# First mixture of experts on gathered 64-row tiles: sixteen by expert, seven for overflow, two side by side

## Chip, cores, metric

One core of a Trainium2 chip runs a whole network forward for one sequence of 256 tokens of width 1024. The metric is the device time of one execution in microseconds (us). Lower is better.

## The reference, cut to what matters

The network is a first block (parallel attention mixer, cross attention to a memory, a hierarchical mixture of experts) and then two layers (a state-space layer and an attention layer), each followed by an expert-choice mixture. The change is in the mixture of the first block:

```python
p_group = jax.nn.softmax((h @ w_group).astype(jnp.float32), axis=-1)      # 4 groups
g_sel = jnp.argmax(p_group, axis=-1)
aff = jax.nn.sigmoid((h @ w_expert)...)                                    # 4 experts in each group
_, local = lax.top_k(aff_grp + bias_grp, TOPK_IN_GROUP)                    # 2 of them
...
for e in range(N_EXPERTS):                                                 # 16, width 256
    act = jax.nn.silu(h @ w_gate[e]) * (h @ w_up[e])
    y = y + combine[..., e:e + 1] * (act @ w_down[e]).astype(jnp.float32)
```

Each token has two experts with a weight above zero, so `combine` has 512 entries above zero out of 256 x 16. h is float32, and so are the weights: 1 MB each for gate, up and down of one expert.

## The kernel before, in words

The kernel is a row of blocks; at the end of each all engines meet. The mixture of the first block has two of them.

**The preparing block** (L1372 to L1515) normalizes X and transposes it into hT (NormT, L423 to L446), computes the router (L1409), works out the choice on VectorE in some 35 small dependent operations (L1462 to L1488), and beside that runs six pieces of an unrelated product, Ada (L763, L751, L783). Then hT is split into a high and a low fp32r part (L458, L461) and the weight of each token for each expert is spread over all partitions as cb by 32 small products (L1420) and eight copies.

**The expert block** (L1529 to L1667) takes every expert over all 256 tokens. Each float32 product is made of three fp32r products of high and low parts, high x low, high x high, low x high (matmul_split, L465 to L467). For one expert, gate_up (L1538) is 2 matrices x 2 halves of the width x 8 chunks of 128 rows x 3 = 96 products of 256 columns; down (L1551) is 2 token tiles x 2 column halves x 2 chunks x 3 = 24 products of 512 columns. PSUM banks Y collect all experts, beginning with X itself (L1535). VectorE splits every weight (L458, L461) and applies cb. SyncE loads the weights of later experts into three slots of 2 MB as old ones come free (L1646, L1652). The block runs as hardware loops over pairs of experts. At the end VectorE copies Y to X (L1635), and SyncE issues the first weights of the state-space block (load_weights, L323) before it reaches the end of the block.

**Helpers.** `Banks` (L101) hands out the eight PSUM banks in turn, and a bank may be filled again when the engine named at its opening has emptied it. `Ring` (L134) does the same for six weight slots of 2 MB: a piece is loaded when the piece before it in its slot has its `freed` mark. SyncE goes through the pieces in one fixed order, and a piece that isn't free yet holds up all behind it. NormT writes each token's normalized row to xn, and then the transposed rows with the gain to hT.

**The expert-choice mixture of the later layers** (L2376 to L2695) isn't changed, but its rows are used below: it already works on gathered tokens, in plain float32 products of 64 columns of stationary data by 512 moving columns, two of them side by side in the two column halves of the array (L2574, `tile_position=(0, 64 * n)`), with its gathering product at L2441 taking every fourth column of xn (`spread`) as stationary data.

Of the kernel before, what the change touches and what calls it, by code (L numbers as in the profile page):

```python
# [13 lines left out]
P = 128  # L14
# [24 lines left out]
CAP = 32  # L39

# [7 lines left out]
def constant_table():  # L48
# [13 lines left out]
    }  # L62
    f = np.float32(10000.0) ** (-np.arange(0, 32, 2, dtype=np.float32) / np.float32(32))
# [3 lines left out]
    parts["cos2d"], parts["sin2d"] = np.cos(ang), np.sin(ang)  # L67
    at, cols = 0, []
# [84 lines left out]
def build(nc, A, out):  # L153
# [15 lines left out]
    with ctx:  # L169
# [90 lines left out]
        gate_v = A["moe_w_gate"].rearrange("a e (k p) n -> p (a e) k n", p=P)  # L260
        up_v = A["moe_w_up"].rearrange("a e (k p) n -> p (a e) k n", p=P)
        down_v = A["moe_w_down"].rearrange("a e (k p) n -> p (a e) k n", p=P)

        weights(("moe1", 0), [(0, KD, D_EXP, gate_v[:, 0]), (2048, KD, D_EXP, up_v[:, 0])], among=3)
        weights(("moe1", 1), [(0, KD, D_EXP, gate_v[:, 1]), (2048, KD, D_EXP, up_v[:, 1])], among=3)
        weights(("moe1", 2), [(2048 * i, 2, D, down_v[:, i]) for i in range(2)], among=3)
        MOE1_SLOTS = [stream[-3 + j][2] for j in range(3)]
# [527 lines left out]
        with ExitStack() as scope:  # L795
# [100 lines left out]
            def _(act):  # L896
                act.dma_start(consts[:, :], A["consts"]).then_inc(ld["consts"], 16)
# [474 lines left out]
        with ExitStack() as scope:  # L1372
            xn = sb("xn3", [P, NT, D], scope=scope)
            wr = sb("wr", [P, KD, 20], scope=scope)
            lg = sb("lg", [P, NT, 20], scope=scope)
            R = {k: sb("r_" + k, [P, NT, 16], scope=scope) for k in ("aff", "score", "w", "one", "both", "m", "d")}
            comb = sb("comb", [P, NT, 16], scope=scope)
            combT = sb("combT", [16, S], scope=scope)
            cb = sb("cb", [P, N_EXP, S], scope=scope)
            gated = sb("gated", [P, 2, 512], scope=scope)  # L1380
            actT = sb("actT", [P, 2, 2, 512], F32R, scope)
            norm = NormT("n3", [X[:, t, :] for t in range(NT)], xn, hT, plain_gain("moe_norm_g"))
            to_combT = Transpose("combT", lambda n, t: comb[:, t, :], 1, 16, lambda g, m: combT[:, :].unsqueeze(1), by=(DVE,))
            wr_loaded, sub_ready, exp_ready, comb_ready = (sem(x) for x in ("wr_loaded", "sub_ready", "exp_ready", "comb_ready"))
            gu_full, silued, act_ready, down_done = (sem(x) for x in ("gu_full", "silued", "act_ready", "down_done"))
            gated_step = sem("gated_step")
            gu_split, down_split = sem("gu_split"), sem("down_split")
            gu_loaded = [sem(f"gu_loaded{j}") for j in range(2)]
            down_loaded = [sem(f"down_loaded{j}") for j in range(2)]
            h_high, h_low = hT_r[:, :, S:2 * S], hT_r[:, :, 0:S]  # L1390
            Y = [psum[i][:, :] for i in range(4)]
            GU = [[psum[4][:, :], psum[5][:, :]], [psum[6][:, :], psum[7][:, :]]]
            prep = scope.enter_context(ExitStack())
            ada_buf = sb("ada_buf3", [P, 2, 512], scope=prep)
            ada0, ada1 = Ada(ada_buf), Ada(ada_buf)
            block = prep.enter_context(nc.Block())

            @block.tensor
            def _(pe):
                ada0.tensor(pe)  # L1400
                norm.tensor(pe)
                pe.wait_ge(wr_loaded, 32)
                for t in range(NT):
                    b = banks.open(("router", t), DVE)
                    if b.emptied:
                        pe.wait_ge(*b.emptied)
# [8 lines left out]
                for e in range(0, N_EXP, 2):  # L1415
                    b = banks.open(("cb", e), (DVE, ACTE)[e // 2 % 2])
                    if b.emptied:
                        pe.wait_ge(*b.emptied)
# [10 lines left out]
            def _(act):  # L1429
# [7 lines left out]
                for e in range(0, N_EXP, 2):  # L1437
                    copy_out(act, ACTE, ("cb", e), cb[:, e:e + 2, :].rearrange("p e t -> p (e t)"), 512)
# [1457 lines left out]
```

## Time and profile before

| | us |
|---|---|
| median of 3 runs | 2513.43 (2509.4 to 2515.15) |
| the profiled execution | 2513.87 |
| its span, first to last instruction | 2512.1 |
| preparing block, from 397 | 42 |
| expert block, to the end of its last product | 281 (439 to 720) |
| last product to the first instruction of the next block | 8.1 |

All rows below are of the profiled execution. PE is the matrix engine's product, PEld its load of stationary data, which overlaps the product before it. DVE is VectorE, ACT ScalarE, SPq the queue of SyncE that issues transfers. A float32 product shows as two records of PE, an fp32r product as one. The duration of a record is longer than the distance between two starts, because the products are pipelined; where the text speaks of a pace, it is the distance. PEclk is the clock granted to the matrix engine as a share of 2.4 GHz: 1.00 is 2.4 GHz, 0.50 is 1.2 GHz.

### The profile page before, as it was taken

What the parts mean: (1) busy time and instruction counts of PE and PEld (TensorE: products, weight loads), DVE (VectorE), ACT (ScalarE), POOL (GpSimd) and SP (SyncE); (2) the same over time, 40 slices, a digit from 0 to 9 for tenths busy, and PEclk for the clock granted to TensorE, in tenths of its full rate; (3) what the DMA queues carried; (4) which work ended last, traced back from release to release, by engine and by line L of the source; (5) the groups of instructions that cost most, each with busy time, mean ns of one, the idle gap of its engine ahead of it and who ended that gap; (6) DMA issues with size and microseconds to landing.
All of it is one profiled execution on the core that took longest, in us unless ns stands there. A gap on an engine that the chain in (4) does not pass through costs nothing. (4 is left out here: it accounts for less than half of the span.)

```text
span 2512.1 us, 27445 instructions
## 1 busy us (share of the span) xinstructions
PE 2153.2 (86%) x10982; PEld 1279.0 (51%) x10982; DVE 1106.7 (44%) x1572; ACT 653.5 (26%) x1197; POOL 43.3 (2%) x55
## 2 busy tenths in 40 slices
PE   7965988999959899999879888888769879888886
PEld 5733444899958788888653222222334433222222
DVE  4576233777757889884431222222247321111112
ACT  4232122000025667674211111111105211111110
POOL 0000000000000000000000000000010000000000
PEclk9968997999988999999979999999889989999998
DMA  8736274455522333332328999999720149999996
GB/s 301 253 116 234 67 291 162 151 200 168 183 71 86 101 119 117 123 113 68 116 119 347 427 428 429 428 429 429 290 100 1 67 172 428 428 429 429 428 429 291
DMA packets 171349, 600.82 MB, mean 239 GB/s; under 512 B 14307, under 2 KB 97638, under 8 KB 144646
## 3 DMA queue, kind: packets, MB, share of 16 engines
q1 hardware_dynamic: 166640, 579.62, 58.9%
q0 software_dynamic: 2352, 16.91, 1.7%
q10 hardware_dynamic: 2278, 3.20, 0.4%
q8 instruction: 54, 0.88, 0.1%
q14 instruction: 25, 0.20, 0.0%
HBM read 598.53 MB, written 1.18 MB: 239 GB/s over the span
## 5 line engine op out<-in xcount | busy, mean ns | idle before, releaser
L2574 PE MATMUL bank<-slots,hT 128*64 128x512 f32 x3072 | 694.6, 599 | 119.8 <-DMA slots<-in_moe_w 87.2
L2574 PEld LDWEIGHTS bank<-slots,hT 128*64 128x64 f32 x3072 | 209.4, 137 | 558.9 <-issue 376.5
L465 PE MATMUL bank<-hT_r,slots_r 128*128 128x256 f32 (+1 forms) x896 | 298.4, 333 | 1.3 <-DVE slots_r L461 1.3
L2654 DVE TENSOR_TENSOR hT<-hT,bank 128x512 f32<-128x512 f32 x32 | 22.0, 687 | 527.4 <-PE bank L2574 527.4
L466 PE MATMUL bank<-slots_r 128*128 128x512 f32 x512 | 200.1, 391 | 0.0
L465 PEld LDWEIGHTS bank<-hT_r,slots_r 128*128 128x128 f32 x896 | 170.6, 190 | 18.4 <-DVE slots_r L461 2.1
L467 PE MATMUL bank<-slots_r 128*128 128x512 f32 x384 | 150.1, 391 | 0.0
L466 PE MATMUL bank<-hT_r,slots_r 128*128 128x256 f32 x512 | 144.8, 283 | 0.0
L467 PE MATMUL bank<-hT_r,slots_r 128*128 128x256 f32 x512 | 144.8, 283 | 0.0
L2635 ACT ACTIVATE hT<-bank 128x512 f32<-128x512 f32 x32 | 19.1, 597 | 450.6 <-PE bank L2574 450.6
L529 PE MATMUL bank<-slots,hT 128*128 128x512 f32 (+1 forms) x320 | 131.5, 572 | 3.9 <-ACT hT L446 2.7
L2658 DVE TENSOR_TENSOR xne<-bank,xne 128x512 f32<-128x512 f32 x32 | 22.1, 691 | 222.6 <-PE bank L2574 222.6
L461 DVE TENSOR_TENSOR slots_r<-slots,slots_r 128x4096 fp32r<-128x4096 f32 (+1 forms) x32 | 107.5, 3359 | 1.1
L466 PEld LDWEIGHTS bank<-slots_r 128*128 128x128 f32 x512 | 96.5, 189 | 20.0
L2639 ACT ACTIVATE hT<-bank 128x512 f32<-128x512 f32 x32 | 19.1, 597 | 324.7 <-PE bank L2608 324.7
L466 PEld LDWEIGHTS bank<-hT_r,slots_r 128*128 128x128 f32 x512 | 98.1, 192 | 0.6
L467 PEld LDWEIGHTS bank<-hT_r,slots_r 128*128 128x128 f32 x512 | 98.1, 192 | 0.0
L529 PEld LDWEIGHTS bank<-slots,hT 128*128 128x128 f32 x320 | 60.5, 190 | 72.8 <-issue 67.0
L2131 DVE SCALAR_TENSOR_TENSOR slots<-slots,vcols 128x512 f32<-128x512 f32 x128 | 95.5, 750 | 3.9 <-ACT slots L1983 0.2
L1779 DVE TENSOR_TENSOR slots_r<-slots,slots_r 128x2048 fp32r<-128x2048 f32 x32 | 73.1, 2285 | 41.9 <-ACT slots_r L1774 41.7
L2666 DVE TENSOR_TENSOR X<-X,bank 128x512 f32<-128x512 f32 x128 | 84.6, 682 | 13.1 <-PE bank L2587 13.1
L458 DVE CAST slots_r<-slots 128x4096 fp32r<-128x4096 f32 (+1 forms) x32 | 56.2, 1757 | 61.7 <-DMA slots<-in_moe_w_up 54.7
(462 smaller groups left out, 3095.9 us busy)
## 6 DMA issues: line engine op xcount, KB each, us to landing
slots<-in_moe_w SPq DMA_DIRECT2D x192, 2048.0 KB, 25.5
slots<-in_ada_w SPq DMA_DIRECT2D x24, 2048.0 KB, 11.5
slots<-in_ssd_in_w SPq DMA_DIRECT2D x48, 512.0 KB, 5.3
slots<-in_moe_w_gate SPq DMA_DIRECT2D x16, 1024.0 KB, 5.5
slots<-in_moe_w_up SPq DMA_DIRECT2D x16, 1024.0 KB, 8.0
slots<-in_moe_w_down SPq DMA_DIRECT2D x16, 1024.0 KB, 5.5
rowsB<-acum_rows POOLq DMA_DIRECT2D x16, 1024.0 KB, 5.8
slots<-in_w_in SPq DMA_DIRECT2D x7, 2048.0 KB, 17.7
```

Source lines behind the costliest of these rows:

```text
L458: return dve.tensor_copy(high, x)
L461: return dve.tensor_tensor(low, x, high.bitcast(F32), ALU.subtract)
L465: pe.matmul(out, lhsT[0], rhs[1], start=start, stop=False, skip_group_check=True)
L466: pe.matmul(out, lhsT[0], rhs[0], start=False, stop=False, skip_group_check=True)
L467: return pe.matmul(out, lhsT[1], rhs[0], start=False, stop=stop, skip_group_check=True)
L529: i = pe.matmul(b.ap[:, 0:width], lhsT(k), rhs(k), start=(k == 0), stop=(k == K - 1))
L1779: dve.tensor_tensor(low_half(w), raw_half(w), high_half(w).bitcast(F32), ALU.subtract).then_inc(w_split, 1)
L2131: i = dve.scalar_tensor_tensor(o, padded[:, c, :, j:j + S], tap(j, CH(g)[c]), o, ALU.mult, ALU.add)
L2574: i = pe.matmul(bank[64 * n:64 * n + 64, :], lhsT(4 * h + k), wv[:, k, n * 512:(n + 1) * 512], start=(h == 0 and k == 0), stop=(h == 1 and ...
L2654: dve.tensor_tensor(acts, sg, psum[1][:, :], ALU.mult).then_inc(a_ready, 1)
L2658: dve.tensor_tensor(ye[j], psum[3][:, :], g2, ALU.mult).then_inc(ye_ready, 1)
L2666: dve.tensor_tensor(res[s_][t][:, c], res[s_][t][:, c], psum[4 + q][:, :], ALU.add).then_inc(sc_added, 1)
```

## The change

- **Sixteen tiles by expert, seven more for overflow.** Each (token, chosen expert) pair is given a place by rank within its expert: the first 64 of an expert go to the 64 rows of the expert's own tile, the others to one of 7 overflow tiles. 23 tiles of 64 rows hold every case, since 512 entries can't fill more than 7 full tiles beyond. The 23 tiles make 12 pairs of 128 rows, the last with one tile.
- **Routing.** The choice gives two one-hot arrays (sel). Ranks come from products with triangular constants (bank "ranks"), and some 14 small DVE operations turn them into places G12, weights W12 and the owner of each overflow tile. rowsG and rowsW hold place and weight of all 512 entries on every partition.
- **Gathering.** xn is split into x_high (ScalarE) and x_low (VectorE, one operation over 2048 elements). For each two pairs ("quad", 6 in all), choose builds a one-hot array of 256 columns, gather makes 4 banks x 2 x 2 x 2 = 32 fp32r products of 256 columns, whose stationary data is every eighth column of x_high or x_low, and take copies them to xg with the gain.
- **Products.** gate_up is 8 chunks x 2 tiles = 16 plain float32 products with 64 stationary and 512 moving columns, gate and up together, the two tiles side by side with different stationary and different moving data. turn is two transposes, down 2 x 2 x 2 = 8 plain products, scatter 8 fp32r products of 512 columns with the one-hot PT, whose result VectorE adds to X.
- **Weights** aren't split. They come as rows of 8 KB, in pieces (pair, 0), (pair, 1) for gate and up of the two tiles and (pair, 2) for both down matrices, through all six slots instead of three. The transfers of the overflow tiles (pairs 8 to 11) take the expert from a register that is loaded from owner_i; there the order is (p, 0), first half of (p, 2), (p, 1), second half of (p, 2).
- Both blocks are one, without hardware loops. Six operations on modcol and ncol move into its first pass, the transfer of C starts in it.

```diff
+CAP1 = 64
+OVER = (2 * S - 1) // CAP1
+TILES = N_EXP + OVER
+PAIRS = (TILES + 1) // 2
...
+        gate_v, up_v, down_v = (A[n].rearrange("a e (p k) n -> p (a e) (k n)", p=P) for n in (
+            "moe_w_gate", "moe_w_up", "moe_w_down"))
+
+        for p in range(PAIRS):
+            mine = [n for n in (2 * p, 2 * p + 1) if n < TILES]
+            if mine[0] == N_EXP:
+                first_overflow = len(stream)
+            for n in mine:
+                weights(("moe1", p, n % 2), [(2048 * m, 1, 2048, v[:, n % N_EXP:n % N_EXP + 1]) for m, v in enumerate((gate_v, up_v))])
+            weights(("moe1", p, 2), [(2048 * (n % 2), 1, 2048, down_v[:, n % N_EXP:n % N_EXP + 1]) for n in mine])
+        after_overflow = len(stream)
...
+                def gather(q):
+                    pe.wait_ge(oh_ready, q + 1)
+                    pe.wait_ge(x_split, 1)
+                    for m in range(KD // 2):
+                        b = banks.open(("xg1", q, m), (DVE, ACTE)[m % 2])
+                        pe.wait_ge(*b.emptied)
+                        for j in range(2):
+                            k = 2 * m + j
+                            for t in range(NT):
+                                for n, x in enumerate((x_high, x_low)):
+                                    i = pe.matmul(b.ap[:, j * 256:(j + 1) * 256], x[:, t, k:D:KD], oh[:, q % 2, t, :],
+                                                  start=(t == 0 and n == 0), stop=(t == NT - 1 and n == 1), skip_group_check=True)
+                        i.then_inc(bank_full, 1)
+
+                def gate_up(p):
+                    b = banks.open(("gu", p), DVE)
+                    pe.wait_ge(*b.emptied)
+                    mine = [(j, ring["moe1", p, j]) for j in range(2) if 2 * p + j < TILES]
+                    for j, piece in mine:
+                        pe.wait_ge(piece.sem, piece.full)
+                    for m in range(2):
+                        g = banks["xg1", p // 2, KD // 2 - 2 + m]
+                        pe.wait_ge(emptied[g.by], g.done)
+                    for k in range(KD):
+                        for j, piece in mine:
+                            at = p % 2 * P + j * CAP1
+                            i = pe.matmul(b.ap[j * CAP1:(j + 1) * CAP1, :].rearrange("p (m n) -> p m n", m=2),
+                                          xg[:, p // 2 % 2, k, at:at + CAP1],
+                                          piece.ap.rearrange("p (m k n) -> p m k n", m=2, k=KD)[:, :, k, :], start=(k == 0),
+                                          stop=(k == KD - 1), tile_position=(0, j * CAP1), skip_group_check=True)
+                    i.then_inc(bank_full, 1)
+                    for j, piece in mine:
+                        piece.freed = (bank_full, b.full)
+
+                def turn(p):
+                    r = rows_of(p)
+                    b = banks.open(("aT1", p), ACTE)
+                    pe.wait_ge(*b.emptied)
+                    pe.wait_ge(emptied[DVE], banks["gu", p].done)
+                    for f in range(2):
+                        i = pe.transpose(b.ap[:, f * P:f * P + r], acts[0:r, p % 2, f:D_EXP:2], consts[0:r, 0:r])
+                    i.then_inc(bank_full, 1)
+
+                def down(p):
+                    piece = ring["moe1", p, 2]
+                    pe.wait_ge(piece.sem, piece.full)
+                    pe.wait_ge(emptied[ACTE], banks["aT1", p].done)
+                    for n in range(2):
+                        b = banks.open(("y1", p, n), DVE)
+                        pe.wait_ge(*b.emptied)
+                        for f in range(2):
+                            for j in range(rows_of(p) // CAP1):
+                                at = 2048 * j + f * D + n * 512
+                                i = pe.matmul(b.ap[j * CAP1:(j + 1) * CAP1, :], aT[:, p % 2, f, j * CAP1:(j + 1) * CAP1],
+                                              piece.ap[:, at:at + 512], start=(f == 0), stop=(f == 1),
+                                              tile_position=(0, j * CAP1), skip_group_check=True)
+                        i.then_inc(bank_full, 1)
+                    piece.freed = (bank_full, b.full)
+
+                def scatter(p):
+                    r = rows_of(p)
+                    pe.wait_ge(PT_ready, p + 1)
+                    pe.wait_ge(emptied[DVE], banks["y1", p, 1].done)
+                    for t in range(NT):
+                        for n in range(2):
+                            b = banks.open(("sc1", p, t, n), DVE)
+                            pe.wait_ge(*b.emptied)
+                            for h, y in enumerate((y_high, y_low)):
+                                i = pe.matmul(b.ap[:, :], PT[0:r, p % 2, t * P:(t + 1) * P], y[0:r, n, :], start=(h == 0),
+                                              stop=(h == 1))
+                            i.then_inc(bank_full, 1)
...
+                gather(0)
+                for p in range(PAIRS + 2):
+                    if p < PAIRS:
+                        gate_up(p)
+                    if p >= 2:
+                        scatter(p - 2)
+                    if 1 <= p <= PAIRS:
+                        down(p - 1)
+                    if p % 2 and p + 1 < PAIRS:
+                        gather((p + 1) // 2)
+                    if p < PAIRS:
+                        turn(p)
...
+                dve.sem_inc(sel_ready, 1)
+                ada1.vector(dve)
...
+                choose(0)
+                dve.wait_ge(x_rounded, 1)
+                dve.wait_ge(bank_full, banks["n3", KD // 2 - 1].full)
+                dve.tensor_tensor(x_low[:, :, :], xn[:, :, :], x_high[:, :, :].bitcast(F32), ALU.subtract).then_inc(x_split, 1)
+                link(dve.tensor_tensor(top, W12[:, 0, :].unsqueeze(2), W12[:, 1, :].unsqueeze(2), ALU.add))
                 link(dve.reciprocal(top, top))
                 link(dve.tensor_tensor(top, top, v["d"][:, :, 2:3], ALU.mult))
-                link(dve.tensor_tensor(comb[:, :, :], v["aff"], top.broadcast_to([P, NT, 16]), ALU.mult))
-                dve.sem_inc(comb_ready, 1)
-                link(split_high(dve, h_high, hT[:, :, 0:S]))
-                link(split_low(dve, h_low, hT[:, :, 0:S], h_high))
-                ada1.vector(dve)
-                to_combT.evacuate(dve, DVE)
-                for e in range(0, N_EXP, 2):
-                    copy_out(dve, DVE, ("cb", e), cb[:, e:e + 2, :].rearrange("p e t -> p (e t)"), 512)
-
-                dve.wait_ge(emptied[DVE], banks["adaT", 23].done)
-                mod = modcol[:, :, :, :, :].rearrange("p l c b s -> p (l c b) s")
-                c = VCOL["ada_b_2"]
-                link(dve.tensor_tensor(mod, mod, vcols[:, c:c + 96].unsqueeze(2).broadcast_to([P, 96, 2]), ALU.add))
-                for l in range(2):
-                    for n, (name, v) in enumerate((("norm1_w_2", 1), ("norm2_w_2", 4))):
-                        c = VCOL[name] + 8 * l
-                        for s_ in range(2):
-                            dve.scalar_tensor_tensor(ncol[:, l, n, s_, :].rearrange("p (a b) -> p a b", a=2),
-                                                     modcol[:, l, 2 * v:2 * v + 2, :, s_], 1.0,
-                                                     vcols[:, c:c + 8].rearrange("p (a b) -> p a b", a=2), ALU.add, ALU.mult)
+                link(dve.tensor_tensor(W12[:, :, :], W12[:, :, :], v["d"][:, :, 0].unsqueeze(1).broadcast_to([P, 2, NT]), ALU.mult))
+                dve.sem_inc(weights_ready, 1)
+                take(dve, DVE, 0)
+                link(dve.tensor_tensor(behind[:, :, :], ends[:, :].unsqueeze(1).broadcast_to([P, OVER, 16]),
+                                       const1("over").unsqueeze(2).broadcast_to([P, OVER, 16]), ALU.is_le))
+                link(dve.tensor_reduce(owner[:, :], behind[:, :, :], AX.X, ALU.add))
+                link(dve.tensor_scalar(owner[:, :], owner[:, :], float(N_EXP - 1), None, ALU.min))
+                dve.tensor_copy(owner_i[:, :], owner[:, :]).then_inc(owner_ready, 1)
+                dve.wait_ge(emptied[ACTE], banks["rowsW"].done)
+                weigh(0)
+                choose(1)
...
+                load_weights(sp, first_overflow)
+                sp.wait_ge(owner_ready, 1)
+                for n in range(OVER):
+                    j, p = n % 2, (N_EXP + n) // 2
+                    e = sp.value_load(owner_i[0:1, n:n + 1], min_val=0, max_val=N_EXP - 1)
+                    piece = ring["moe1", p, j]
+                    sp.wait_ge(*piece.before.freed)
+                    for m, table in enumerate((gate_v, up_v)):
+                        sp.dma_start(piece.ap[:, 2048 * m:2048 * (m + 1)], table[:, e]).then_inc(piece.sem, 16)
+                    piece = ring["moe1", p, 2]
+                    if j == 0:
+                        sp.wait_ge(*piece.before.freed)
+                    sp.dma_start(piece.ap[:, 2048 * j:2048 * (j + 1)], down_v[:, e]).then_inc(piece.sem, 16)
+                issued[0] = after_overflow
```

## Rows read from the trace of the kernel before

**Rows 1.** Windows view: us, busy time of each engine (instructions), granted clock, transfers.
```profile
core 0: us, PE busy (x) PEld busy (x) DVE busy (x) ACT busy (x) POOL busy (x), PEclk, DMA share, GB/s
...
410.00:424.00 14.00, 7.98 (x65) 3.02 (x64) 10.47 (x41) 3.40 (x6) 0.00 (x0) 0.94 0.80 260
424.00:439.00 15.00, 14.02 (x32) 10.46 (x32) 3.80 (x14) 2.39 (x4) 0.00 (x0) 0.50 0.47 179
439.00:446.00 7.00, 5.50 (x9) 2.14 (x9) 6.79 (x3) 0.00 (x0) 0.00 (x0) 0.72 0.43 150
446.00:720.00 274.00, 273.79 (x1920) 256.08 (x1920) 194.40 (x127) 19.83 (x24) 0.00 (x0) 1.00 0.48 161
```

**Rows 2.** Source view of the expert block's transfers: duration, first and last start; landing.
```profile
L1646 SPq DMA_DIRECT2D slots<-in_moe_w_gate x14: 368/373/392, 457.8 to 674.6; - x14
...
DMA to landing us min/median/max: 4.8/5.5/7.3
```

**Rows 3.** Timeline of PE in the expert block: start us, duration, line, form.
```profile
446.21 0.28 PE L466 MATMUL bank<-hT_r,slots_r 128*128 128x256 f32 x1
446.33 0.28 PE L467 MATMUL bank<-hT_r,slots_r 128*128 128x256 f32 x1
...
718.92 0.40 PE L465 MATMUL bank<-slots_r,actT 128*128 128x512 f32 x1
719.15 0.40 PE L466 MATMUL bank<-slots_r,actT 128*128 128x512 f32 x1
```

**Rows 4.** Timeline of PE, first expert-choice mixture: side by side products, at its start and later.
```profile
1323.79 8.63 PE L2574 MATMUL bank<-slots,hT 128*64 128x512 f32 x32 [2.63 <-ACT hT L2629]
...
1411.85 3.65 PE L2574 MATMUL bank<-slots,hT 128*64 128x512 f32 x16 [1.24 <-DMA slots<-in_moe_w]
```

**Rows 5.** Windows view, inside the same mixture: columns as in Rows 1.
```profile
1430.00:1530.00 100.00, 83.47 (x394) 25.97 (x394) 19.01 (x30) 10.70 (x22) 0.00 (x0) 1.00 1.01 428
```

**Rows 6.** Timeline of PE, Ada: four products side by side, each with its own stationary data.
```profile
410.21 3.64 PE L763 MATMUL bank<-slots,scT 128*32 128x512 f32 x32
```

**Rows 7.** Source view, loads of stationary data (ns min/median/max): contiguous, every fourth column.
```profile
L466 PEld LDWEIGHTS bank<-hT_r,slots_r x512: 187/192/192, 446.1 to 708.1; 128*128 128x128 f32 x171
...
L2441 PEld LDWEIGHTS bank<-hT,xne x96: 307/308/338, 1287.0 to 2034.8; 128*128 128x128 f32 x96
```

**Rows 8.** Timeline of the preparing block and the first products after it.
```profile
418.37 0.19 DVE L1483 TENSOR_TENSOR r_both<-r_both,r_w 128x32 f32<-128x32 f32 x1
421.04 2.29 DVE L461 TENSOR_TENSOR hT_r<-hT,hT_r 128x2048 fp32r<-128x2048 f32 x1
445.98 0.39 PE L465 MATMUL bank<-hT_r,slots_r 128*128 128x256 f32 x1 [1.27 <-DVE slots_r L461]
```

**Rows 9.** Windows view, after the pause of PE: columns as in Rows 1.
```profile
441.00:443.00 2.00, 2.00 (x4) 0.88 (x3) 1.97 (x2) 0.00 (x0) 0.00 (x0) 0.53 1.00 408
443.00:445.00 2.00, 1.71 (x4) 0.41 (x3) 2.00 (x1) 0.00 (x0) 0.00 (x0) 1.00 0.18 72
```

**Rows 10.** Timeline: operations of the forms that the change adds, in other places.
```profile
452.12 1.28 ACT L1582 ACT_TABLE_LOAD   x1 [13.34 <-PE bank L467]
...
765.09 0.42 DVE L2180 SCALAR_TENSOR_TENSOR slots<-slots 128x256 f32<-128x256 f32 x1
...
767.88 0.29 DVE L2184 TENSOR_SCALAR slots<-slots 128x256 f32<-128x256 f32 x1
...
1779.37 0.68 DVE L2666 TENSOR_TENSOR X<-X,bank 128x512 f32<-128x512 f32 x1
```

**Rows 11.** Timeline around the end of the expert block.
```profile
719.82 2.48 DVE L1635 COPY X<-bank 128x512 f32<-128x512 f32 x4 [8.45 <-PE bank L467]
...
727.93 0.38 ACTq L2028 DMA_DIRECT2D w_dt<-in_ssd_in_w  x1
...
724.00 3.52 SPq L323 DMA_DIRECT2D slots<-in_ssd_in_w  x2
```

More of the change, by code:

```diff
@@ L67, in constant_table @@
     parts["cos2d"], parts["sin2d"] = np.cos(ang), np.sin(ang)
+    parts.update(sparse)
     at, cols = 0, []
@@ L1372, in build @@
         with ExitStack() as scope:
+            xn_base = (nc.sbuf_base + 31) // 32 * 32
             xn = sb("xn3", [P, NT, D], scope=scope)
+            x_low = nc.alloc_sbuf_tensor_at("xn3_r", [P, NT, D], F32R, offset=xn_base)
+            x_high = sb("x_high3", [P, NT, D], F32R, scope)
             wr = sb("wr", [P, KD, 20], scope=scope)
             lg = sb("lg", [P, NT, 20], scope=scope)
-            R = {k: sb("r_" + k, [P, NT, 16], scope=scope) for k in ("aff", "score", "w", "one", "both", "m", "d")}
@@ L1384, in build @@
[L1384 to L1396, printed above, removed]
+            R = {k: sb("r_" + k, [P, NT, 16], scope=scope) for k in ("aff", "score", "one", "both", "m", "d")}
@@ new lines, in build @@
+            consts1 = sb("consts1", [P, CONSTS["slot_of"][1] - CONSTS["lead"][0]], scope=scope)
+            gain1 = sb("gain1", [P, KD], scope=scope)
+            sel = sb("sel1", [P, 2, NT, 16], scope=scope)
+            selm = sb("selm1", [P, 2, NT, 16], scope=scope)
+            ranks = sb("ranks1", [P, 48], scope=scope)
+            tiles, ends, starts = (sb(x, [P, 16], scope=scope) for x in ("tiles1", "ends1", "starts1"))
+            place = sb("place1", [P, NT, 16], scope=scope)
+            G12, W12 = (sb(x, [P, 2, NT], scope=scope) for x in ("G12", "W12"))
@@ new lines, in _ @@
+                link(dve.tensor_reduce(W12[:, :, :], selm[:, :, :, :], AX.X, ALU.add))
+                b = banks["ranks"]
+                dve.wait_ge(bank_full, b.full)
+                dve.tensor_copy(ranks[:, :], b.ap[:, 0:48]).then_inc(emptied[DVE], 1)
+                dve.wait_ge(emptied[DVE], b.done)
+                dve.wait_ge(consts1_loaded, 32)
+                rank, count = ranks[:, 0:32].rearrange("p (t e) -> p t e", t=NT), ranks[:, 32:48]
+                link(dve.tensor_scalar(tiles[:, :], count, CAP1 + 0.5, None, ALU.is_gt))
@@ new lines, in _ @@
+                for n in range(2, S // CAP1):
+                    link(dve.scalar_tensor_tensor(tiles[:, :], count, n * CAP1 + 0.5, tiles[:, :], ALU.is_gt, ALU.add))
+                link(dve.tensor_tensor_scan(ends[:, :], const("ones")[:, 0:16], tiles[:, :], 0.0, ALU.mult, ALU.add))
+                link(dve.tensor_tensor(starts[:, :], ends[:, :], tiles[:, :], ALU.subtract))
+                link(dve.scalar_tensor_tensor(starts[:, :], starts[:, :], float(CAP1), const1("lead"), ALU.mult, ALU.add))
```

337 lines of the change are left out of this document (171 added, 166 removed).

## The prediction

> **What bounds the kernel now.** I read the windows view first, for the part that the change touches. In the expert block PE is busy for 273.79 of 274 us at full clock while the transfers move 161 GB/s [rows 1]. So the matrix engine sets this stage, and its length is a count of products times their pace. The source view of the weight transfers gives the period: the first fourteen gate matrices are asked for between 457.8 and 674.6 us [rows 2]; 216.8 us for 13 experts, 16.7 us each, the first gap a short one. The timeline's pace gives the same: 96 products 0.12 us apart and 24 products 0.235 us apart are 11.5 + 5.6 = 17.1 us of products [rows 3]. Ahead of it lies a preparing part in which no engine is full but which is a chain: after the choice is made at 418.56 us come the split of hT, 32 small products at half clock for 14.02 us (one window of 15) and the first splits of weights, so that the first expert product starts at 445.98 [rows 1, 8]. Behind it, the last product is followed by a copy at 719.82 and the next block begins only at 727.93, because SyncE was still issuing small-row transfers until 724.00 + 3.52 [rows 11]. What follows (state-space layer and later) begins with ScalarE's squares of X and isn't touched; I take its length as it is.
>
> **What the change costs per pair.** The nearest relative of the new products is the later mixture. There a float32 product of 64 stationary by 512 moving columns has two records; 16 records, so 8 products, take 3.65 us including the last one's tail of 0.2, which makes 0.43 us per product, or 0.855 per two side by side [rows 4]. At M = 64 two run for the time of one.
> - gate_up: 8 x 0.855 = 6.84 us for two tiles. down: 4 x 0.855 = 3.42. scatter: 8 fp32r products at 0.235 = 1.88 [rows 3]. turn: two transposes, taken at 0.45 with their tail.
> - gather, once for two pairs: 32 fp32r products of 256 columns. Their pace would be 0.12 [rows 3] if the stationary data came as fast as there, but it is every eighth column. A contiguous load is recorded at 192 ns while products follow at 120, every fourth column at 308 ns [rows 7]. If the part that overlaps (192 - 120 = 72) stays the same, the pace with a stride is 308 - 72 = 236 ns, and gather is 32 x 0.236 = 7.55 us. No row shows a stride of eight. Lower end: 0.12, 3.8 us. Upper end: the excess over contiguous doubles again, about 0.35 to 0.40, 12 us. I take 0.236, since it is the nearest row.
> - After gather, the next gate_up waits for the last bank's copy by ScalarE or VectorE, two operations of about 0.42, with a signal: 0.8 us.
>
> So an even pass is 6.84 + 1.88 + 3.42 + 0.45 = 12.6 us, and an odd one with gather 12.6 + 7.55 + 0.8 = 20.9. The other engines stay under that: per pass VectorE has four additions to X of 0.6 to 0.7 [rows 10], two y_low of 0.65, gate, PT, weigh and half of choose and take, some 8 to 9 us; ScalarE about 3. In each pass the wait for silu and gate before turn (some 1.2 us) lies behind scatter and down, 5.3 us of PE work. The float32 products need no split weights, so the 194 us of VectorE in this stage fall to about 100.
>
> **Sum of the loop.** Pass 0 has no cover: gate_up 6.84, a table load 1.28 [rows 10], silu and gate 0.4 each, turn 0.45, signals: 10.0. Pass 1: 19.0 (no scatter). Passes 2, 4, 6, 8, 10 and 11: 6 x 12.6 = 75.6. Passes 3, 5, 7, 9: 4 x 20.9 = 83.6. The tail (scatter, down, rounding and y_low uncovered 1.6, scatter, last additions): 9.7. Together 198 us.
>
> **Weights.** 23 tiles x 3.15 MB = 72 MB, where 16 experts were 50. At the 428 GB/s that the later mixture reaches [rows 5] a pair's 6.3 MB take 14.7 us, while the mean pass is 16.8: under the pace, with little air. Up to pair 7 this holds, as (p, 0) and (p, 1) are asked for when gate_up(p-2) is done. From pair 8 on the order is another: SyncE waits for down(p-2) before the first half of (p, 2), and (p, 1) stands behind it. From the end of down(p-2) it is 1 + 2 MB at 428 GB/s (7.35), a fixed part of about 2.6 (a 1 MB transfer lands after 5.5 [rows 2], of which 2.45 is the move) and 1 for issues and register load: 10.9 us until gate_up(p) may start. Then gate_up, scatter and down(p-1), 12.1, so a period of 23.0 for 12.6 or 20.9 of work. Gate_up(8) comes 3 us late, gate_up(9), whose pass before is a short one, 10.6, gate_up(10) 2.4: **16 us** of waits. Pair 11 has one tile and no such wait. No row shows what a register load on SyncE costs; I bound it by 0 and 3 us each, of which only three are exposed, and by the later mixture's loops, whose registers don't show in the pace, I take it near 0.5.
>
> **Ahead of the loop.** From 418.56: Ada's three reductions and two operations on weights 0.9, ranks on PE (10 records) beside that, then copy and 12 small operations at 0.22 = 2.9, to place_ready at 423.3; GQ and choose(0), 2 x 0.29 + 2 x 0.42 [rows 10] plus waits, 1.9; x_low 2.29, as the split of hT [rows 8]; four small operations 0.9; so weights_ready at 428.4. rowsW on PE at half clock, 8 records, 1.8: gather(0) starts at 430.2. Its first four us run at 1.2 GHz: after the last pause the first products from 439 on ran at 0.50, and by 443 it was 1.00 [rows 9]. That costs 2 us: 430.2 + 7.55 + 2, and 1.3 for take: **gate_up(0) at 441.1**, where the first expert product was at 445.98. x_high (1.9) goes into ScalarE's idle time before the exponential. The first two pairs' 12 MB start near 400 instead of 412, since all six slots are used, and are there by 432. The moved operations on modcol stand behind gate(0) on VectorE, 1 us with 8 us of air.
>
> **Behind it.** The state-space weights of slot 0 are free after down(10), about 8 us before the end, so SyncE has issued its six small-row transfers (7.7 us [rows 11]) by then. The next block starts 0.3 after the last addition instead of 8.1 after the last product.
>
> **Clock.** The pause before gate_up(9) is over 10 us. A pause of PE ahead of 424 brought the clock to 0.50 [rows 1], so I add 2 us for the climb. The Trainium skill ("TensorE: Matmul & The Clock Gate", HAM oscillation) describes a thin kernel that falls back to half clock at every wait for weights. By it each pass that waits would pay such a climb.
>
> **Total.** 441.1 + 198 + 16 + 2 + 0.3 = 657.4, for 727.93: 70.5 us less. 2513.87 - 70.5 = **2443 us**; the median shown is 0.4 below the profiled execution, which changes nothing.
>
> **Rivals.**
> - **The gather is cheap or the order of overflow loads harmless.** For it: 72 ns of overlap may grow for strided loads. At 0.12 the passes are bound by transfers in turn (14.7), and the loop ends 11 us earlier: 2432, inside the range. With the waits from pair 8 gone too, 2411. Beyond the range's lower end 8%.
> - **The gather is dearer, or passes hide less than I think.** At 0.40 the loop ends 27 us later: 2470; with 1 us more of signal waits in each pass 2482. It would show as a long gap between gather's loads. Beyond the upper end 11%.
> - **Clock lost at each wait.** In the later mixture 32 records from a cold start took 8.63 us, while later ones kept 3.65 for 16 and waits of 1.24 us left the clock at 1.00 [rows 4, 5]. So 1.5 us per pass, 12 passes: +18, less the 2 counted, 2459. That is the page's rule on these waits; the trace speaks against it for short ones. 4%, inside the range.
> - **Slower: side by side doesn't overlap.** In L2574 both products use the same stationary data; here each has its own. If two of them took 2 x 0.855, gate_up and down would be 20.5 instead of 10.3 in each pass: + 123 us, 2566. It turns to slower from 0.57 of that excess (70.5 / 123) on. Against it: Ada's 32 records in 3.64 us, 0.11 each, are four column groups with different stationary data and overlap fourfold [rows 6]. 2%.
> - **It doesn't do what it says.** If places or weights were computed but PE's count of tiles didn't fall: the count is fixed in code at 23 tiles, so only the loop's waits could eat it, which is the second rival.
>
> **How the numbers follow.** My case and the clock case hold 79%, below 8%, above 11%, slower 2%. The range runs from 2426 (gather at 0.12 and 6 us fewer waits) to 2464 (gather at 0.31, +10, and 11 us of more waits, or the clock case with 5). Faster by over 0.2% (5 us, about what a measurement of this kernel can tell): 97%, within 1%, slower 2%.
>
> **What would show it.** Products with two records of 64 columns at 0.43 per product; gather's loads at about 308 ns and 0.236 apart; gate_up(0) near 441; passes of 12.6 and 20.9 in turn; a wait of PE on in_moe_w_gate or in_moe_w_up of 10 us once and 2 to 3 twice, late in the stage and nowhere before; the next block at 657, with no gap behind the last addition. I am wrong if even passes take over 14 us (overlap or VectorE), if the weights make passes before pair 8 wait (rows of 8 KB slower than rows of 16), or if the stages behind 728 move by more than a us or two.

## Result, and the profile after

| | before | after |
|---|---|---|
| median | 2514.29 us (2509.4 to 2516.85, 4 runs) | 2448.09 us (2444.16 to 2450.41, 4 runs) |
| ratio | | 0.9737, 95% interval 0.9716 to 0.9758 |
| span of the profiled execution | 2512.1 | 2448.0 |

2443 was forecast, in a range of 2426 to 2464. The change takes 66 us off the median, 64.1 off the profiled span. To split these, I measure in both traces from the first transfer of the preparing block (wr, 397.15 and 394.43 us):

| us | before | after | forecast |
|---|---|---|---|
| to the first product with expert weights | 48.8 | 42.0 | 44.0 |
| from there to the first instruction of the next block | 282.0 | 228.3 | 216.3 |
| all that follows | 1784.2 | 1783.3 | 1784.2 |
| all ahead of the preparing block | 397.15 | 394.43 | 397.15 |

So the part that was changed gained 60.5 us where 70.5 were forecast. The 2.7 us ahead of it aren't the change's: the run with the corrected overflow order had that point at 391.54, the one with both edits at 396.50.

PE's timeline of the kernel after (start, duration, engine, line, form, count; in brackets the idle time before) has the new passes in it, two without and with gather, and the late ones:
```profile
466.18 7.09 PE L1462 MATMUL bank<-slots,hT 128*64 128x512 f32 x32 [0.77 <-ACT hT L1565]
...
475.24 3.65 PE L1489 MATMUL bank<-slots,aT 128*64 128x512 f32 x16
478.83 0.51 PE L1476 MATMUL bank<-consts,acts 128*128 128x128 f32 x2
479.26 7.09 PE L1462 MATMUL bank<-slots,hT 128*64 128x512 f32 x32
...
492.27 0.41 PE L1446 MATMUL bank<-oh,xn_r 128*128 128x256 f32 x1
492.51 0.40 PE L1446 MATMUL bank<-oh,x_high 128*128 128x256 f32 x1
...
500.93 7.09 PE L1462 MATMUL bank<-slots,hT 128*64 128x512 f32 x32 [0.77 <-ACT hT L1565]
...
535.68 8.78 PE L1462 MATMUL bank<-slots,hT 128*64 128x512 f32 x32 [0.77 <-ACT hT L1565]
...
574.82 9.76 PE L1462 MATMUL bank<-slots,hT 128*64 128x512 f32 x32 [3.47 <-issue]
...
600.72 8.76 PE L1462 MATMUL bank<-slots,hT 128*64 128x512 f32 x32 [10.08 <-issue]
...
625.27 8.43 PE L1462 MATMUL bank<-slots,hT 128*64 128x512 f32 x32 [2.01 <-issue]
```
gate_up's 32 records take 7.09 us, with their tail; that is the pace of [rows 4], where 16 took 3.65. An even pass, 466.18 to 479.26, takes 13.08 us, an odd one, 479.26 to 500.93, 21.67. Gather's products follow each other at 0.24 us. PE waits 3.47, 10.08 and 2.01 us before gate_up(8), (9) and (10), 15.6 together; and in four passes of this list gate_up takes 8.4 to 9.8 us instead of 7.09.

Gather's loads of stationary data (source view; ns min/median/max, first and last start), which answer to [rows 7]:
```profile
L1446 PEld LDWEIGHTS bank<-oh,x_high x96: 312/337/342, 427.4 to 622.2; 128*128 128x128 f32 x96
```

The timeline of SyncE's queue around gate_up(9), columns as in the timeline of PE:
```profile
566.43 0.34 SPq L1773 DMA_DIRECT2D slots<-in_moe_w_gate  x1
566.87 0.39 SPq L1773 DMA_DIRECT2D slots<-in_moe_w_up  x1
590.25 0.33 SPq L1777 DMA_DIRECT2D slots<-in_moe_w_down  x1
591.34 0.34 SPq L1773 DMA_DIRECT2D slots<-in_moe_w_gate  x1
591.78 0.38 SPq L1773 DMA_DIRECT2D slots<-in_moe_w_up  x1
592.25 0.39 SPq L1777 DMA_DIRECT2D slots<-in_moe_w_down  x1
```
From 566.87 to 590.25 SyncE asks for nothing, though slots have been free since gate_up(7) ended at 557.5. At 590.25, when down(7) is done, come the first half of (9, 2) and then, at 591.34, the gate weights of tile (9, 1), on which gate_up(9) waits till 600.72.

The end of the stage, which answers to [rows 11]:
```profile
663.75 0.69 DVE L1733 TENSOR_TENSOR X<-X,bank 128x512 f32<-128x512 f32 x1 [0.17 <-PE bank L1504]
...
664.73 0.39 ACTq L2142 DMA_DIRECT2D w_dt<-in_ssd_in_w  x1
...
652.45 7.64 SPq L339 DMA_DIRECT2D slots<-in_ssd_in_w  x6
```
The six small-row transfers are issued by 660.1, and the next block begins 0.3 us after the last addition.

### The profile page after: what moved, and what is told of

Same layout as the page of the kernel before. It is cut to its first block and busy times, and to the rows that moved or that the text cites. A ratio compares the mean times of both kernels' runs of the same rounds, so it can differ in the third digit from the quotient of the medians.

```text
span 2448.0 us, 25235 instructions
## 1 busy us (share of the span) xinstructions
PE 2078.0 (85%) x9910; PEld 1128.2 (46%) x9910; DVE 997.9 (41%) x1633; ACT 667.6 (27%) x1245; POOL 43.3 (2%) x55
## 5 line engine op out<-in xcount | busy, mean ns | idle before, releaser
L2688 PE MATMUL bank<-slots,hT 128*64 128x512 f32 x3072 | 696.4, 599 | 117.4 <-DMA slots<-in_moe_w 86.7
L2688 PEld LDWEIGHTS bank<-slots,hT 128*64 128x64 f32 x3072 | 212.0, 137 | 555.6 <-issue 372.2
L481 PE MATMUL bank<-hT_r,slots_r 128*128 128x512 f32 x384 | 153.6, 400 | 0.0
L1462 PE MATMUL bank<-slots,hT 128*64 128x512 f32 x368 | 94.1, 649 | 18.9 <-issue 15.5
L482 PEld LDWEIGHTS bank<-slots_r 128*128 128x128 f32 x512 | 96.5, 188 | 19.9
L545 PEld LDWEIGHTS bank<-slots,hT 128*128 128x128 f32 x320 | 60.5, 190 | 72.8 <-issue 67.0
L2780 DVE TENSOR_TENSOR X<-X,bank 128x512 f32<-128x512 f32 x128 | 84.5, 681 | 13.1 <-PE bank L2701 13.1
L2701 PE MATMUL bank<-xne 32*128 32x512 f32 x384 | 75.4, 665 | 8.1 <-DVE X L2780 8.1
L481 PEld LDWEIGHTS bank<-hT_r,slots_r 128*128 128x128 f32 x384 | 72.4, 189 | 15.6 <-issue 1.2
L483 PEld LDWEIGHTS bank<-slots_r 128*128 128x128 f32 x384 | 72.3, 188 | 15.5
L2114 ACT ACTIVATE rowsB<-rowsB,nb 128x128 f32<-128x128 f32 x256 | 76.4, 391 | 2.2 <-DVE rowsB L2368 2.2
L1888 ACT ACTIVATE slots_r<-slots 128x2048 fp32r<-128x2048 f32 x32 | 61.0, 1907 | 51.1 <-PE bank L483 51.1
L1462 PEld LDWEIGHTS bank<-slots,hT 128*64 128x64 f32 x368 | 31.4, 149 | 73.0 <-issue 72.4
## 6 DMA issues: line engine op xcount, KB each, us to landing
slots<-in_moe_w_gate SPq DMA_DIRECT2D x23, 1024.0 KB, 10.8
```

What stands on the lines that cost most here:

```text
L481: pe.matmul(out, lhsT[0], rhs[1], start=start, stop=False, skip_group_check=True)
L482: pe.matmul(out, lhsT[0], rhs[0], start=False, stop=False, skip_group_check=True)
L483: return pe.matmul(out, lhsT[1], rhs[0], start=False, stop=stop, skip_group_check=True)
L545: i = pe.matmul(b.ap[:, 0:width], lhsT(k), rhs(k), start=(k == 0), stop=(k == K - 1))
L1462: i = pe.matmul(b.ap[j * CAP1:(j + 1) * CAP1, :].rearrange("p (m n) -> p m n", m=2), xg[:, p // 2 % 2, k, at:at + CAP1], piece.ap.rearrang ...
L1888: act.activation(high_half(w), raw_half(w), ACT.Copy).then_inc(w_rounded, 1)
```

## The experiments

Stage lengths below run from the start of gate_up(0) to the start of gate_up(11), which leaves out what varies ahead of the stage: 203.3 us in the kernel after.

**Are the late waits a matter of order?** In the overflow transfers both registers are loaded first, then (p, 0), (p, 1), then (p, 2):
```diff
-                for n in range(OVER):
...
-                    if j == 0:
-                        sp.wait_ge(*piece.before.freed)
+                for p in range(N_EXP // 2, PAIRS):
+                    mine = [n for n in (2 * p, 2 * p + 1) if n < TILES]
+                    e = [sp.value_load(owner_i[0:1, n - N_EXP:n - N_EXP + 1], min_val=0, max_val=N_EXP - 1) for n in mine]
+                    for j in range(len(mine)):
...
+                    piece = ring["moe1", p, 2]
                     sp.wait_ge(*piece.before.freed)
```


> The changed kernel, with the order of the overflow transfers put back to that of the first pairs: (p, 0), (p, 1), then both halves of (p, 2), with the registers of both tiles loaded first. Theory 1 (the waits before gate_up(8), (9) and (10), 3.5 + 10.1 + 2.0 = 15.6 us, come from (p, 1) standing behind the wait for down(p-2)): the waits go, and with them some 4 to 6 us of half clock after them, so 17 to 21 us less than the changed kernel, 2427 to 2431. Rival (register loads and the 72 MB themselves set the late passes): the waits stay at 5 us or more each, at most 6 us less, 2442 or more.


Measured: 2428.51 us, ratio to before 0.9662 (0.9626 to 0.9697); stage 183.6 us. PE's timeline:
```profile
569.38 7.09 PE L1462 MATMUL bank<-slots,hT 128*64 128x512 f32 x32 [0.77 <-ACT hT L1565]
...
582.47 7.09 PE L1462 MATMUL bank<-slots,hT 128*64 128x512 f32 x32
...
604.13 7.09 PE L1462 MATMUL bank<-slots,hT 128*64 128x512 f32 x32 [0.77 <-ACT hT L1565]
```
gate_up(8), (9) and (10) start 0.77 us after turn or without a wait, and take 7.09 us each: of the 15.6 us of waits 14.0 are gone (the 0.77 for ScalarE's copy of the gathered rows stays twice), and with them 5.7 of half clock (2.7, 1.7 and 1.3 in the three passes). That is 19.7, and the stage is 19.7 shorter. Theory 1 stands. The bandwidth was there.

**Does the stride set gather's pace?**
```diff
-                                    i = pe.matmul(b.ap[:, j * 256:(j + 1) * 256], x[:, t, k:D:KD], oh[:, q % 2, t, :],
+                                    i = pe.matmul(b.ap[:, j * 256:(j + 1) * 256], x[:, t, k * P:(k + 1) * P], oh[:, q % 2, t, :],
...
-                act.activation(x_high[:, :, :], xn[:, :, :], ACT.Copy).then_inc(x_rounded, 1)
+                act.activation(by_k(x_high), by_row(xn), ACT.Copy).then_inc(x_rounded, 1)
```
(by_k and by_row view a row as 8 chunks of 128 and as 128 groups of 8; x_low is written the same way.)


> The changed kernel, with x_high and x_low written in the order of the chunks, so that gather's stationary data is contiguous; x_low has a buffer of its own. Theory 2 (a load of every eighth column takes 337 ns where a contiguous one takes 190, and sets gather's pace of 0.24): the pace falls to 0.12, gather from 7.7 to 3.9 us; four gathers lie outside the late waits, so 15 us less, and 3 more if gate_up(0) and gate_up(6) no longer run partly at half clock: 2430 to 2434. Gathers in passes 7 and 9 give nothing, as transfers are waited for there. Rival (the transfers, 14.7 us for each pass, take over at once): 8 us less, 2440. Rival (the pace has another cause, 256 columns against the new data): nothing, 2448.


Measured: 2437.02 us, 0.9708 (0.9672 to 0.9743); stage 193.0, 10.3 less, and each gather half as long:
```profile
L1448 PEld LDWEIGHTS bank<-oh,x_high x96: 186/188/333, 426.1 to 604.8; 128*128 128x128 f32 x96
L1448 PE MATMUL bank<-oh,x_high x96: 277/281/561, 426.2 to 605.0; 128*128 128x256 f32 x96
```
So the load was the cause of the pace: 188 ns again, and gather(1) lies within a pass 1 of 15.5 us, not 19.45. But the gain is between the theory (15 to 18) and the rival that the transfers take over (8). In the stage, part of it comes back as new waits of 2.3 and 1.9 us at gate_up(5) and (7). The waits before gate_up(8) and (10) grow from 3.5 to 7.6 and from 2.0 to 5.8 us, by what gather gives up in the passes before them, as expected. Ahead of the stage nothing is gained: the permuted x_high and x_low take 3.94 and 3.84 us instead of 1.91 and 2.29, gather(0) starts 2.2 us later after the transfer of wr, and gate_up(0) starts 42.0 us after it in both kernels.

**Both edits.**


> Both edits: order of overflow transfers and contiguous stationary data. Passes would be 13.1 and 17.8 in turn, mean 15.4, against 14.7 us of transfers. If the effects add up: 15 to 21 from the order, 26 from six gathers and the clock, 38 to 45 us less: 2403 to 2410. Rival (transfers set the pace from the third pair on): 30 us less, 2418, with waits of PE on in_moe_w in most passes.


Measured: 2414.4 us, 0.9615 (0.9582 to 0.9648), stage 165.5; once more beside the runs of the last experiment, 2416.47, 0.9606 (0.9583 to 0.9628). 34 us less than the kernel after, between the two expectations. gate_up(5), (7) and (9) still wait 1.3 to 2.0 us.

**Whose are these waits?** SyncE asks for gate and up of pair p only after down of pair p - 1, which waits for down(p - 3); but gate_up(p - 2), which frees their slots, ends 5.3 us before that. The order of pieces was changed for the whole stage, in the overflow transfers too:
```diff
+        gate_up_weights(0)
+        for p in range(1, PAIRS):
+            if 2 * p == N_EXP:
                 first_overflow = len(stream)
+            gate_up_weights(p)
+            down_weights(p - 1)
+        down_weights(PAIRS - 1)
```


> Contiguous stationary data, and all transfers of the stage in the order in which the slots come free: gate and up of pair p before down of pair p - 1, since gate_up(p - 2) ends 5.3 us before down(p - 3). Theory 4 (with both edits the stage loses some 8 us to gate_up(5), (7) and (9) waiting for transfers that SyncE asks for only after down, while the transfers as such need 14.7 us per pass): the waits go, 4 to 8 us less than with both edits alone, 2406 to 2410. Rival (the transfer rate itself is the limit): no change, 2414 within 2.

> The changed kernel with the same order of all transfers, stationary data strided as it is. Theory (with strided data PE has air in each pass and only the overflow order was at fault): equal to the run with the overflow order alone, 2428 within 3. Rival (an earlier request helps by itself): 3 or more less.

> Both edits once more, beside the two above on the same chip: 2414 within 3.


Measured: with contiguous data 2407.1 us, 0.9573 (0.9552 to 0.9594), 9.4 less than both edits alone on the same chip; with strided data 2430.43, 0.9666 (0.9644 to 0.9688), as with the overflow order alone. The windows view (us, busy times, clock, share, GB/s) of both edits alone, then of the new order:
```profile
462.00:590.00 128.00, 119.73 (x590) 57.68 (x589) 62.81 (x119) 21.56 (x48) 0.00 (x0) 1.00 0.95 389
```
```profile
462.00:590.00 128.00, 124.91 (x618) 58.96 (x616) 62.81 (x118) 21.56 (x48) 0.00 (x0) 1.00 1.00 414
```
The same 128 us carry 389 GB/s and 119.73 us of PE, then 414 GB/s and 124.91. In the stage PE waits for no weights any more, and the first gate transfer of a pair is asked for as soon as the slot is free: at 468.15, when gate_up(2) ends at 468.12, where in both edits alone it was asked for 6.5 us after that end (476.65 and 470.14). Theory 4 stands, with a smaller size than the medians say. The stage went from 165.8 to 160.5 us, 5.3 less, about what gate_up(4), (5), (7) and (9) had waited beyond the 0.77 for a copy. The rest of the 9.4 lies outside the stage, where the two profiled executions of both edits alone already differ by 5.3 us, so nothing here shows that it is the edit's. 2407.1 is the best version of this study, 4.3% under the kernel before, and in that window both PE and the transfers are nearly full.

**Would rows of 1 KB have done?** Layout of gate and up as in the kernel before, which makes gather contiguous for nothing:
```diff
-        gate_v, up_v, down_v = (A[n].rearrange("a e (p k) n -> p (a e) (k n)", p=P) for n in (
...
+        gate_v, up_v = (A[n].rearrange("a e (k p) n -> p (a e) k n", p=P) for n in ("moe_w_gate", "moe_w_up"))
```


> The changed kernel with the layout of gate and up weights of the kernel before (rows of 1 KB, chunk by chunk) and thus contiguous stationary data in gather without another buffer. Theory (rows of 1 KB come about as fast, since 2 MB landed after 7.3 us in the kernel before): same as with packed x, 2430 to 2434. Rival (small rows are slower, and the stage with its 5 MB per 15 to 17 us has no air for it): transfers late in every pass, 2445 to 2470.

> Order of overflow transfers put right and the 1 KB layout of gate and up with contiguous stationary data. If rows of 1 KB are as fast as rows of 8 KB: as with both edits on packed x, 2403 to 2410. If they are slower: later by what the rows cost in each of the 12 passes, 2415 to 2450.


Measured: 2449.91 us, 0.9742 (0.9709 to 0.9775), stage 204.9, so 12 more than with packed x; with the overflow order 2423.72, 0.9644 (0.9622 to 0.9667), stage 177.5, again 12 more than the stage with both edits. The windows of the first, around gate_up(3) and (4):
```profile
460.00:476.00 16.00, 13.21 (x60) 5.52 (x61) 8.46 (x15) 2.27 (x6) 0.00 (x0) 1.00 1.05 350
476.00:495.00 19.00, 18.60 (x90) 9.65 (x90) 7.31 (x16) 3.03 (x7) 0.00 (x0) 0.91 1.06 367
```
The transfer engines are full (share 1.05) at 350 to 367 GB/s, where rows of 16 KB gave 428 [rows 5] and rows of 8 KB, in a window of 16 us of both edits, 422. Only gate and up have rows of 1 KB; down, a third of the bytes in these windows, still has 8 KB. The rival stands: with 1 KB rows the stage's transfers are slower by about a sixth, and it has no air for it. They are late in every second pass, by 2.5, 2.6 and 3.2 us before gate_up(3), (5) and (7).

**Do two products run side by side?** gate_up goes tile by tile:
```diff
-                    for k in range(KD):
-                        for j, piece in mine:
+                    for j, piece in mine:
+                        for k in range(KD):
```


> The changed kernel with gate_up's products ordered tile by tile (all eight chunks of tile 0, then of tile 1) instead of alternating. Output is the same. Theory (the pace of 0.43 per product comes from two neighbours in different column halves running together): gate_up of the 11 full pairs takes 13.7 instead of 7.1 us, 6.7 more in each; of these 75 us some 20 fall into the late waits, so 50 to 60 us more, 2500 to 2508. Rival (the engine finds the partner within its queue, or the pace has nothing to do with the neighbour): no change, 2448.


Measured in a single run: 2503.98 us; stage 259.2, 55.9 longer. The same products:
```profile
475.99 12.26 PE L1462 MATMUL bank<-slots,hT 128*64 128x512 f32 x32 [0.77 <-ACT hT L1565]
```
12.26 us where alternating order takes 7.09. Neighbours in different column halves do run together, each with its own stationary data. It is 12.3 and not 13.7, so some products still overlap where the second tile's begin.

**What do the seven overflow tiles cost?**
```diff
-TILES = N_EXP + OVER
+TILES = N_EXP
```


> The changed kernel with the sixteen tiles by expert alone; entries beyond the 64th of an expert are left out of the sum. Shows what the seven overflow tiles cost. Theory: passes 8 to 11 go, that is from the end of gate_up(7)'s pass to gate_up(11)'s, about 571 to 652 less nothing at the tail, 75 to 80 us less: 2368 to 2373. Rival (the tail of the stage or the next stage waits for something else): 60 or less.


Measured in a single run: 2357.51 us, 90.6 under the kernel after. From gate_up(0) to the next block it is 139.0 instead of 228.3 us. 89 us, not 75 to 80: I had left out gather(4), which stands in pass 7 (7.7). A part of it is the late waits; the rest is 4 passes of products and 22 MB.

**Whose was the gap in the kernel before?** One `load_weights(sp)`, at the end of its expert block (L1665), was left out, so that the next block issues these transfers.


> The kernel before with one line left out: SyncE doesn't issue the first state-space weights at the end of the expert block, but in the next block. Theory 3 (the 5.6 us between the last copy and the next block are SyncE's six small-row transfers ahead of the block's end): the gap falls to 0.4 us, 4 to 5 us less than the kernel before, unless ScalarE then waits for the first half of weights. Rival (the gap is code fetched after a hardware loop): nothing gained, 0 or a few us more.


Measured: 2507.18 us, ratio to before 0.9976 (0.9964 to 0.9989, 10 runs), 6 us less than 2513.14. The end of its expert block:
```profile
720.02 2.48 DVE L1635 COPY X<-bank 128x512 f32<-128x512 f32 x4 [8.45 <-PE bank L467]
722.75 9.22 SPq L323 DMA_DIRECT2D slots<-in_ssd_in_w  x6
722.77 0.46 ACTq L2027 DMA_DIRECT2D w_dt<-in_ssd_in_w  x1
```
The next block begins 0.3 us after the copy, in spite of the hardware loop before it. The gap was the queue of SyncE, and 5 of the 66 us could have been had without the change.

## Why the prediction was right, point by point

2443 was 5 us from the median, and part of that closeness is luck. The part that the change touches gained 10 us less than forecast; 2.7 us ahead of it and 0.9 behind it came on top of that, and the medians lie 2.1 us further apart than the profiled spans. What was right is the mechanism: fewer products at the pace of side by side ones, a gather paced by its loads, and late waits from the order of the overflow transfers. What was wrong in size is mostly the clock.

The passes, in us (forecast, with its own waits; measured from start to start of gate_up):

| pass | 0 | 1 | 2 | 3 | 4 | 5 | 6 | 7 | 8 | 9 | 10 | 11 to next block |
|---|---|---|---|---|---|---|---|---|---|---|---|---|
| forecast | 10.0 | 19.0 | 12.6 | 20.9 | 12.6 | 20.9 | 12.6 | 23.9 | 23.2 | 23.3 | 12.6 | 22.6 |
| measured | 10.3 | 19.5 | 13.1 | 21.7 | 13.1 | 21.7 | 14.8 | 24.4 | 25.9 | 24.6 | 14.4 | 25.0 |

- **Pace of side by side products: right.** 7.09 and 3.65 us as taken from [rows 4]; that different stationary data don't hinder it was shown by taking the alternation away.
- **Products of an even pass: 0.5 low.** I counted each group of products by its pace and left out what lies between groups: scatter begins with a record of 0.50 and its second 0.34 us behind, and with turn it is the same. 12.6 should have been 13.1 in every even pass, and the odd ones come out 0.5 to 0.8 longer too: 6.0 us over passes 1 to 10, waits and clock taken off. The run with the overflow order alone has the same 13.1 and 21.7 in passes without a late wait.
- **Gather: right, for the reason given, its number by luck.** 0.236 forecast, 0.24 measured. The load takes 337 ns, not 308, but 337 - 240 = 97 of it overlap, not 72. The estimate had both wrong by about the same amount, and the errors cancel. Contiguous data bring 0.12.
- **Late waits: right, and 2 us less.** 3, 10.6 and 2.4 were forecast on top of the 0.8 for the copy after gather. Measured are 3.5, 10.1 and 2.0, of which the copy has 0.77 in the first and the last: 2.7, 10.1 and 1.2, together 14.0 where 16 stood. They are gone with the order. The working has two slips: 5.5 less 2.45 is 3.05 and not 2.6, and a period of 23.0 against passes of 20.9, 12.6 and 20.9 makes 2.1, 10.4 and 2.1, so 14.6 and not 16. The register loads fall into the bound: from the issue of a down half at 590.25 to the next gate at 591.34 it is 1.1 us, where neighbours are 0.4 to 0.5 apart.
- **Clock: mis-sized.** I added 2 us for one pause. The granted clock was at 0.50 after all three late waits, 3.5 and 2.0 us long ones too, which cost 2.7, 1.7 and 1.3 us. And gate_up(0) and gate_up(6), with no wait but 0.8 to 1.0 us, ran partly at half clock, 1.7 each. So the terms of the clock were 9.1 us, where 2 stood. The rule of the Trainium skill ("TensorE: Matmul & The Clock Gate", HAM oscillation) that a thin kernel falls back at its waits for weights held for each late wait of this kernel; I had judged it by the later mixture, where waits of 1.24 us left the clock at 1.00 [rows 4, 5]. It doesn't hold for each wait of the other runs. Waits of 2.3 us in the run with contiguous data, of 2.0 and 2.2 in the two of both edits, and of 3.2 and 3.0 before gate_up(7) in the two with 1 KB rows were followed by 7.09 us at full clock. Waits of 2.4 to 2.6 before gate_up(3) and (5) of those last two were followed by 8.4 to 8.8. So the length of the wait alone doesn't decide it, and what does stays open. Two passes of the run with 1 KB rows:
```profile
475.94 8.78 PE L1462 MATMUL bank<-slots,hT 128*64 128x512 f32 x32 [2.50 <-issue]
...
546.81 7.09 PE L1462 MATMUL bank<-slots,hT 128*64 128x512 f32 x32 [3.18 <-issue]
```
Windows of the kernel after, columns as in [rows 1]:
```profile
436.40:438.40 2.00, 2.00 (x6) 0.74 (x8) 1.72 (x5) 1.14 (x1) 0.00 (x0) 0.62 0.05 20
...
535.60:537.60 2.00, 1.92 (x6) 0.83 (x8) 0.95 (x2) 0.20 (x1) 0.00 (x0) 0.56 1.03 430
539.60:541.60 2.00, 2.00 (x12) 0.81 (x10) 0.00 (x0) 0.00 (x0) 0.00 (x0) 1.00 0.98 406
...
574.80:577.00 2.20, 2.18 (x6) 0.84 (x8) 0.00 (x0) 0.00 (x0) 0.00 (x0) 0.50 1.01 428
```
- **Preparing part: 2 us better.** 42.0 instead of 44.0. The chain up to gather was right: x_low ended at 424.85 and gather(0) began at 427.43, 30.4 and 33.0 us after the transfer of wr, where 30.3 and 33.1 were forecast. What was wrong are the 2 us for a start at half clock. The clock was at 0.50 from 427.40 to 430.00 and at 0.99 from there to 434.00, and the strided products follow each other at 0.24 us in both stretches, so half clock cost next to nothing here:
```profile
428.75 0.44 PE L1446 MATMUL bank<-oh,xn_r 128*128 128x256 f32 x1
428.99 0.44 PE L1446 MATMUL bank<-oh,x_high 128*128 128x256 f32 x1
...
432.31 0.41 PE L1446 MATMUL bank<-oh,x_high 128*128 128x256 f32 x1
432.55 0.41 PE L1446 MATMUL bank<-oh,xn_r 128*128 128x256 f32 x1
```
- **End: right.** The gap is gone for the reason named. The tail is 2.4 us longer than forecast: a wait of 1.08 and one of 1.44 us for y_low, of which 1.6 were counted, and the last scatter partly at half clock (records of 0.63). Clock 7.1, products 6.0 and end 2.4, less 1.4 in pass 0 and 2.0 in the late waits, are the 12 us by which the stage is longer than forecast.
- **VectorE and ScalarE: right.** VectorE is busy for 5.4 us in an even pass of 13 and 10.8 in an odd one of 22, and no wait in the passes names it but turn(0).
- **Rivals.** The slower one fell with the experiment on alternation. That the transfers would take over when gather is cheap was in the forecast for 0.12, as 11 us less than mine. The run with contiguous data alone gave 11 less than the kernel after, but that the two agree is luck: 3.4 of its 10.3 us in the stage are half clock that is gone, a term the forecast didn't have. The 2411 named for cheap gather without late waits doesn't follow from the terms, as 2432 less 16 and less 2 of clock is 2414; both edits measured 2414.4.

## What to carry to other kernels

A queue that asks for transfers in a fixed order should have them in the order in which their places come free; one wait in front of pieces that were free earlier cost 20 us here, and 5 more in the stage once the rest was fast. When weights are gathered per tile, look at the stride of the stationary operand: as long as products of 256 columns follow closely, its load sets the pace. And before an edit of hundreds of lines look at what SyncE issues ahead of the end of a block: one line gave 6 us.

## What the runs showed of the hardware that I hadn't expected

- A strided load of 128 stationary columns in fp32r takes 337 ns at every eighth column, 308 in float32 at every fourth [rows 7], 188 when contiguous; products of 256 columns then follow at 0.24 us instead of 0.12. Between a step of four and one of eight lie only 29 ns, with the type different too.
- At half clock the stride costs little. In gather(0) at a clock of 0.50 the strided loads take 340 ns and the products follow at 0.24 us; the contiguous ones of the packed run take 330 ns (the 333 in its view) and follow at 0.21.
- After strided gathers the clock was found at half in gate_up(0) of all five runs with strided data that have it (8.78 or 8.79 us in four, 13.96 instead of 12.3 in the tile by tile one), and in three of them in gate_up(6). In the six runs with contiguous data it was at full clock in gate_up(0), after the same wait of 1.02 us. That the stride is the cause isn't shown: gate_up(2) and (4) follow the same strided gathers after waits of 0.77 us, and ran in 7.09 us in each of the four alternating runs.
- Transfers in which rows of 1 KB carry two thirds of the bytes fill the engines at 350 to 367 GB/s. Rows of 8 KB reach 422 over 16 us, and 428 and 430 in two of the short windows of the kernel after shown above, and so are no slower than rows of 16 KB at 428.
